# Start of a hybrid encoder step: value weights on a second DMA queue, tile 0 rounded first, identity transposes on PE

## The chip, the cores and the metric

One core of a Trainium2 chip runs the whole program. The metric is the device time in microseconds (us) of one execution, taken as the median of several runs. Engines: PE is TensorE (matrix multiply), ACT is ScalarE, DVE is VectorE, POOL is GpSimd; SP is the sync engine, which here only issues DMAs. A "q" behind an engine's name is its instruction queue.

## What is computed

One layer of a streaming encoder over 1024 prompt tokens and 8 x 16 sample tokens (1152 rows of 1024 features, float32):

```python
def rms_norm(x, w):
    y = xf * lax.rsqrt(jnp.mean(xf * xf, axis=-1, keepdims=True) + EPS)
    return (y * w).astype(x.dtype)

xn = rms_norm(x, norm_w)
h, gb, gc, q, k, v, g_conv, g_attn = jnp.split(xn @ w_in, SPLITS, axis=-1)
...   # q, k: rms_norm per head; short gated convolution of gc * h; sliding-window attention
x = x + merged @ w_out
x = x + (silu(rms_norm(x, w_ffn) @ w_gate) * (rms_norm(x, w_ffn) @ w_up)) @ w_down
```

The change touches only the first some 50 us: the first `rms_norm`, and v, the 256 value columns of `xn @ w_in`.

## The kernel before, in words

The 1152 rows are nine token tiles of 128 rows (`NT = 9`); the 1024 features are eight blocks of 128 (`KT = 8`). Every float32 product is made of three matmuls on operands split into a rounded high part and a remainder (`PASSES`: high x high, high x low, low x high). So every operand is split: ACT makes the high part by a rounding copy, then POOL (weights) or DVE (tokens) subtracts it from the source to make the low part.

Each engine has its own instruction list, in the order written in its block, and the lists meet in semaphores alone. The head of the program, by engine:

- **SP** (lines 371 to 388) issues the loads: x tile 0, the norm weight broadcast to all partitions (`wbc_p`, line 381), value-weight half 0 (`v_half(Slab(0))`, two DMAs of 256 KB into `raw0`), x tile 1, value-weight half 1 (two DMAs into `raw1`), x tiles 2 to 8, then the key weights (`cols`), which wait for a raw buffer to come free. An x tile is 128 rows of 4 KB. A value-weight DMA is 128 partitions x 2 rows of 1 KB. The norm weight is one row of 4 KB, read once for each partition.
- **ACT** (lines 701 to 726): one square root that loads its table (line 703); `norm_stats(0, t)` for a tile is its squares with their sum (line 682) and a root (line 686); `split_hi(Slab(n))` rounds weight half n (line 671); `norm_hi_part(t)` rounds a transposed tile out of PSUM in two halves (line 698); `v_rows(t)` copies a finished value tile (line 711). The order is stats 0, weight half 0, stats 1, then for each t: round tile t, stats t + 2, (at t = 0) weight half 1, and from t = 2 a value copy.
- **DVE** (lines 1006 to 1013): `norm_scale(0, t)` multiplies tile t by 1/rms and the norm weight (lines 989, 995), `norm_lo_part(t)` makes the low part (line 1004). Tiles 0 and 1 are scaled first.
- **POOL**: constants (lines 472 to 485; `consts_made` counts to 11), then `split_lo` of weight halves 0 and 1 (line 490), then small DMAs.
- **PE** (lines 1431 to 1449): `norm_transpose(t)` transposes a normalised tile by eight matmuls against the identity (line 1404, into banks 5 to 7), `v_unit(t, half)` is 12 matmuls of tile t against one weight half (line 1414, bank `t % DU`, `DU = 5`). Tiles 0 and 1 are transposed, then for each t both value halves (tile 0's second half waits for `w_lo >= 2`), and the transposes of tile t + 2. The last four tiles take their second halves afterwards (`V_LATE = 4`). Behind come keys, queries, attention, convolution, output projection (line 1618) and the feed-forward part (lines 1674, 1716).

The normalised tiles have two buffers (`xn_p`), and transposed halves rotate over three banks (`norm_bank`).

Of the kernel before, what the change touches and what calls it, by code (L numbers as in the profile page):

```python
# [32 lines left out]
P = 128  # L33
# [4 lines left out]
NT = TOK // P  # L38
NG = 3
G = TOK // NG  # L40
KT = D // P
HD = 64
NH, NKV = D // HD, 4
NV = NKV * HD
# [7 lines left out]
V_OFF = K_OFF + NKV * HD  # L52
# [19 lines left out]
PASSES = ((0, 0), (0, 1), (1, 0))  # L72

DU = 5

PAIRS = 2 * NCH
RING = 8
# [51 lines left out]
def norm_bank(t, h):  # L129

    return 5 + (2 * t + h) % 3
# [11 lines left out]
def build(nc, io):  # L143
    ctx = ExitStack()
    with ctx:
        def sb(name, shape, dt=F32):
            return ctx.enter_context(nc.sbuf_tensor(name, shape, dt))

        def sem(name):
            return ctx.enter_context(nc.semaphore(name))  # L150
# [56 lines left out]
        raw = [raw0, raw1]  # L207
# [4 lines left out]
        ident = sb("ident", [P, P])  # L212
# [28 lines left out]
        banks = ctx.enter_context(nc.psum_tensor("banks", [P, 8, 512], F32))  # L241
# [5 lines left out]
        raw_in = [sem("raw_in0"), sem("raw_in1")]  # L247
        cache_in = [sem("cache_in0"), sem("cache_in1")]
        wbc_in = sem("wbc_in")
# [33 lines left out]
        w_in = io["w_in"][0].rearrange("(k p) c -> p k c", p=P)  # L283
# [14 lines left out]
        def slab_is_done(eng, kind, idx):  # L298
            if kind == "u":
                eng.wait_ge(gemm_ready, idx)  # L300
            elif kind == "du":
                eng.wait_ge(d_ready, idx)
            elif kind == "f":
                eng.wait_ge(gemm_ready, 3 * (idx + 1))
            else:
                eng.wait_ge(d_ready, NT * (idx + 1))
# [51 lines left out]
        def _(sp):  # L358
            def load(slab, halves_of):


                if not (isinstance(slab.n, int) and slab.n < 2):
                    sp.wait_ge(w_lo, slab.n - 1)
                for dst, src in halves_of:
                    sp.dma_start(dst, src).then_inc(raw_in[slab.slot], 16)
# [5 lines left out]
            def x_tile(t):  # L371
                sp.dma_start(X[:, t, :], xp[t] if t < NT - 1 else xsm).then_inc(x_in[t], 16)

            def v_half(slab):

                k0 = slab.n * KT // 2
                load(slab, [(raw[slab.slot][:, k * NV:(k + 2) * NV].rearrange("p (k c) -> p k c", k=2),
                             w_in[:, k0 + k:k0 + k + 2, V_OFF:V_OFF + NV]) for k in (0, 2)])

            x_tile(0)  # L380
            sp.dma_start(wbc_p[:, :], io["norm_mix_w"][0].partition_broadcast(P)).then_inc(wbc_in, 16)
            v_half(Slab(0))
            x_tile(1)
            v_half(Slab(1))
            for t in range(2, NT):
                x_tile(t)
            cols(Slab(2), w_in, K_OFF)
            cols(Slab(3), w_in, K_OFF + P)
            with sp.Fori(0, 2) as i:
                for j in range(4):  # L390
                    slab = Slab(Q_SLAB + j, 4, i)
# [273 lines left out]
        def _(act):  # L665
            def split_hi(slab, *free):
                act.wait_ge(raw_in[slab.slot], 32 * (slab.turn + 1))
                if free:

                    slab_is_done(act, *free)  # L670
                act.activation(ws[slab.slot][0][:, :], raw[slab.slot][:, :], ACT.Copy).then_inc(w_hi, 1)  # L671

            def norm_squares(ph, t):

                if ph == 0:
                    act.wait_ge(x_in[t], 16)
                else:

                    act.wait_ge(d_free, LAST_BASE + LAST_POS[1, t] + 1)
                act.wait_ge(sq_done, (NT + 6) * ph + t + 1)  # L680
                scratch = scratch_p[:, :] if ph == 0 else junk[:, :] if t < 4 else xn_f[:, 0, :]
                act.activation(scratch, X[:, t, :], ACT.Square, accum_out=ss[:, t:t + 1]).then_inc(sq_done, 1)

            def norm_roots(ph, t0, t1):
                act.wait_ge(sq_done, (NT + 6) * ph + t1 + 1)
                act.activation(sd[:, t0:t1], ss[:, t0:t1], ACT.Sqrt, bias=eps[:, :], scale=1.0 / D).then_inc(sd_done, t1 - t0)

            def norm_stats(ph, t):
                norm_squares(ph, t)
                norm_roots(ph, t, t + 1)  # L690

            def norm_hi_part(t):

                for h in range(2):
                    idx = 2 * t + h
                    act.wait_ge(nT_done, idx + 1)
                    src = banks[:, norm_bank(t, h), :].rearrange("p (k c) -> p k c", k=4)
                    act.activation(xs[0][:, 4 * h:4 * h + 4, t * P:(t + 1) * P], src, ACT.Copy).then_inc(norm_hi, 1)


            act.wait_ge(consts_made, 11)

            act.activation(sd[:, 0:1], eps[:, :], ACT.Sqrt).then_inc(sq_done, 1)
            norm_stats(0, 0)
            split_hi(Slab(0))
            norm_stats(0, 1)

            def v_rows(t):

                act.wait_ge(v_ready, t + 1)  # L710
                act.activation(V[:, 1 + t, :], banks[:, t % DU, 0:NV], ACT.Copy).then_inc(v_done, 1)

            for t in range(NT):
                norm_hi_part(t)
                if t + 2 < NT:
                    norm_stats(0, t + 2)
                if t == 0:
                    split_hi(Slab(1))
                if 2 <= t < NT - V_LATE + 2:
                    v_rows(t - 2)  # L720

# [261 lines left out]
        def _(dve):  # L983
            def norm_scale(ph, t):

                xn, wbc = ((xn_p, wbc_p), (xn_f, wbc_f))[ph]
                q = NT * ph + t
                dve.wait_ge(sd_done, q + 1)
                dve.reciprocal(rms[:, t:t + 1], sd[:, t:t + 1]).then_inc(rms_done, 1)
                if ph == 0 and t >= 2:  # L990
                    dve.wait_ge(nT_done, 2 * (t - 1))
                if ph == 1 and t >= 2:
                    dve.wait_ge(tr_done, 2 * (t - 1))
                dve.wait_ge(rms_done, q + 1)
                dve.scalar_tensor_tensor(out=xn[:, t % 2, :], in0=X[:, t, :], scalar=rms[:, t:t + 1], in1=wbc[:, :],
                                         op0=ALU.mult, op1=ALU.mult).then_inc(xn_ready, 1)

            def norm_lo_part(t):
                for h in range(2):
                    idx = 2 * t + h  # L1000
                    dve.wait_ge(norm_hi, idx + 1)
                    src = banks[:, norm_bank(t, h), :].rearrange("p (k c) -> p k c", k=4)
                    where = (slice(None), slice(4 * h, 4 * h + 4), slice(t * P, (t + 1) * P))
                    dve.tensor_tensor(xs[1][where], src, xs[0][where].bitcast(F32), ALU.subtract).then_inc(norm_lo, 1)

            dve.wait_ge(wbc_in, 16)
            norm_scale(0, 0)
            norm_scale(0, 1)

            for t in range(NT):  # L1010
                norm_lo_part(t)
                if t + 2 < NT:
                    norm_scale(0, t + 2)
            dve.wait_ge(const_in, 16 * 15)
# [176 lines left out]
            def add_rows(s, hf, x_turn=None):  # L1191
                for t in range(NT):
# [4 lines left out]
                    else:  # L1197

                        dve.wait_ge(d_free, NT * (s - 2) + t + 1)
                    dve.tensor_tensor(x, banks[:, 3 + t % DU, :], x, ALU.add).then_inc(d_free, 1)  # L1200

# [176 lines left out]
        def _(pe):  # L1378
# [17 lines left out]
            def norm_transpose(t):  # L1396
                pe.wait_ge(xn_ready, t + 1)
                for h in range(2):
                    idx = 2 * t + h
                    if idx >= 3:  # L1400
                        pe.wait_ge(norm_lo, idx - 2)
                    for k in range(4):
                        kt = 4 * h + k
                        mm = pe.transpose(banks[:, norm_bank(t, h), k * P:(k + 1) * P],  # L1404
                                          xn_p[:, t % 2, kt * P:(kt + 1) * P], ident[:, :])
                    mm.then_inc(nT_done, 1)
# [3 lines left out]
            def v_unit(t, half):  # L1410

                for k in range(KT // 2):
                    for n, (w, x) in enumerate(PASSES):
                        mm = pe.matmul(banks[:, t % DU, 0:NV], xs[x][:, 4 * half + k, t * P:(t + 1) * P],  # L1414
                                       ws[half][w][:, k * NV:(k + 1) * NV],
# [12 lines left out]

            norm_transpose(0)
            norm_transpose(1)
            for t in range(NT):
                pe.wait_ge(norm_lo, 2 * (t + 1))
                if t >= DU:
                    pe.wait_ge(v_done, t - DU + 1)
                if t < 2:
                    pe.wait_ge(w_lo, 1)
                mm = v_unit(t, 0)
                if t < NT - V_LATE:  # L1440
                    if t == 0:
                        pe.wait_ge(w_lo, 2)
                    v_unit(t, 1).then_inc(v_ready, 1)
                elif t == NT - 1:
                    mm.then_inc(v_half_used, 1)
                if t + 2 < NT:
                    norm_transpose(t + 2)
            for t in range(NT - V_LATE, NT):
# [174 lines left out]
            def row_units(slot, s, act_slot):  # L1623
                for t in range(NT):

                    if t >= DU:
                        pe.wait_ge(d_free, NT * s + t - DU + 1)
# [129 lines left out]
```

## Time and profile before

| | us |
|---|---|
| Median of 3 runs | 1736.22 |
| Lowest, highest | 1735.95, 1737.91 |
| The profiled execution's own time | 1736.17 |
| Its span in the profile | 1734.4 |

Busy times in the span: PE 1693.8 us, its weight loads (PEld, beside the matmuls) 1598.8, DVE 891.4, POOL 876.8, ACT 649.2.

How to read it: times of rows are counted from the span's start. "Busy" is the time in which an engine works; an engine waits idle for a semaphore, and a row names what released it behind an arrow. The chain of waits is followed back from the last instruction: at each step to what released it, or to the instruction before it on its engine. A DMA's time to landing runs from its issue to its last byte. The DMA share is the mean busy share of the core's 16 DMA engines, PEclk the clock granted to TensorE.

### The profile page before, as it was taken

The numbers are of one execution on the slowest core, as the hardware profiler recorded it, in microseconds if no ns is written. First come the engines' busy times: TensorE is split into PE (matmuls) and PEld (weight loads), VectorE is DVE, ScalarE is ACT, GpSimd is POOL, SyncE is SP. The second block draws the span as 40 slices with busy tenths as digits, with TensorE's granted clock in tenths as the row PEclk, the third lists the DMA queues.
The fourth block names the chain that finished last, engine by engine and source line by source line (L and its number), as shares of the span: only waits on it lengthen the run. The fifth ranks groups of instructions, "written<-read, shape, count | busy, mean of one in ns | idle before, by whom it ended". The sixth has DMA issues, their size and how long they took to land.

```text
span 1734.4 us, 29336 instructions
## 1 busy us (share of the span) xinstructions
PE 1693.8 (98%) x10942; PEld 1598.8 (92%) x10942; DVE 891.4 (51%) x1537; ACT 649.2 (37%) x1354; POOL 876.8 (51%) x779
## 2 busy tenths in 40 slices
PE   7999999999999999999998999999979999999999
PEld 7999999989999999999887999999969999999998
DVE  5400465536554313312567756657677555565555
ACT  6221555535554211111115454444434333333331
POOL 3412555345552221212235887887848665666662
PEclk9999999999999999999999999999989999999999
DMA  5221111111111111114120334333323223222222
GB/s 172 51 47 48 41 35 35 30 32 48 34 35 32 37 49 37 48 36 155 41 85 25 98 99 121 97 99 97 98 73 122 80 91 98 74 74 74 95 77 85
DMA packets 143155, 121.66 MB, mean 70 GB/s; under 512 B 33202, under 2 KB 124750, under 8 KB 143024
## 3 DMA queue, kind: packets, MB, share of 16 engines
q1 hardware_dynamic: 130400, 115.89, 21.6%
q10 hardware_dynamic: 11984, 3.61, 0.9%
q8 instruction: 81, 1.33, 0.3%
q0 software_dynamic: 640, 0.43, 0.1%
q14 instruction: 50, 0.41, 0.1%
HBM read 114.58 MB, written 5.32 MB: 69 GB/s over the span
## 4 chain that ended last, share of the span: by engine, by line
PE 84%; issue 9%; DVE 3%; POOL 3%; ACT 1%; DMA 0%; SPq 0%; POOLq 0%; DVEq 0%; ACTq 0%
PE banks L1674 28%; PE banks L1391 27%; PE banks L1716 15%; PE banks L1618 5%; PE banks L1560 2%; PE banks L1542 2%; PE banks L1414 1%; POOL w_lo L490 1%; PE banks L1522 1%; PE banks L1567 1%; DVE xc_lo L1245 1%; PE banks L1489 1%; DMA X<-in_x_prompt 0%; PE banks L1531 0%; PE banks L1404 0%
## 5 line engine op out<-in xcount | busy, mean ns | idle before, releaser
L1391 PE MATMUL banks<-x_hi,w_hi 128*128 128x384 f32 x1200 | 412.2, 344 | 0.0
L1391 PE MATMUL banks<-x_hi,w_lo 128*128 128x384 f32 x1200 | 401.8, 335 | 0.0
L1391 PE MATMUL banks<-x_lo,w_hi 128*128 128x384 f32 x1200 | 401.5, 335 | 0.0
L490 POOL TENSOR_TENSOR w_lo<-w_raw,w_hi 128x1024 fp32r<-128x1024 f32 x44 | 113.2, 2573 | 428.9 <-ACT w_hi L671 428.8
L1674 PE MATMUL banks<-xc_hi,ring_a 128*128 128x256 f32 (+1 forms) x1200 | 247.2, 296 | 0.0
L1391 PEld LDWEIGHTS banks<-x_hi,w_hi 128*128 128x128 f32 x1200 | 225.9, 188 | 5.1
L1391 PEld LDWEIGHTS banks<-x_lo,w_hi 128*128 128x128 f32 x1200 | 225.6, 188 | 0.8
L1391 PEld LDWEIGHTS banks<-x_hi,w_lo 128*128 128x128 f32 x1200 | 225.3, 188 | 0.0
L636 POOL TENSOR_TENSOR ring_a<-raw_f,ring_a 128x512 fp32r<-128x512 f32 x133 | 191.5, 1453 | 19.0 <-ACT ring_a L899 17.8
L1674 PEld LDWEIGHTS banks<-xc_hi,ring_a 128*128 128x128 f32 x1200 | 196.4, 190 | 0.4
L1674 PE MATMUL banks<-xc_lo,ring_a 128*128 128x256 f32 (+1 forms) x600 | 177.7, 296 | 0.0
L1329 DVE TENSOR_TENSOR X<-banks,X 128x512 f32<-128x512 f32 x198 | 128.5, 683 | 42.4 <-PE banks L1716 42.4
L1716 PE MATMUL banks<-ring_a,h_act 128*128 128x512 f32 x618 | 144.0, 391 | 1.0 <-DVE X L1329 1.0
L1674 PE MATMUL banks<-xc_hi,ring_o 128*128 128x256 f32 (+1 forms) x640 | 136.8, 300 | 5.2 <-DVE xc_lo L1245 5.2
L1716 PEld LDWEIGHTS banks<-ring_a,h_act 128*128 128x128 f32 x618 | 114.9, 188 | 25.9 <-issue 1.4
L636 POOL TENSOR_TENSOR ring_a<-w_sums,ring_a 128x512 fp32r<-128x512 f32 x63 | 87.6, 1390 | 84.5 <-ACT ring_a L899 84.5
L671 ACT ACTIVATE w_hi<-w_raw 128x1024 fp32r<-128x1024 f32 x60 | 63.4, 1056 | 153.3 <-PE banks L1391 89.8
L1674 PEld LDWEIGHTS banks<-xc_lo,ring_a 128*128 128x128 f32 x600 | 113.9, 190 | 0.4
L1674 PEld LDWEIGHTS banks<-xc_hi,ring_o 128*128 128x128 f32 x640 | 107.5, 193 | 5.8 <-DVE xc_lo L1245 5.6
L899 ACT ACTIVATE ring_a<-raw_f 128x512 fp32r<-128x512 f32 x133 | 81.6, 624 | 78.3 <-PE banks L1716 58.6
L800 ACT ACTIVATE probs<-banks,soft,rs 128x256 f32<-128x256 f32 x144 | 79.7, 562 | 63.6 <-DVE soft L1061 63.5
L636 POOL TENSOR_TENSOR ring_o<-raw_f,ring_o 128x512 fp32r<-128x512 f32 x66 | 93.3, 1423 | 8.7 <-ACT ring_o L899 8.3
(222 smaller groups left out, 3256.7 us busy)
## 6 DMA issues: line engine op xcount, KB each, us to landing
w_raw<-in_w_in SPq DMA_DIRECT2D x104, 256.0 KB, 3.2
raw_f<-in_w_gate SPq DMA_DIRECT2D x88, 256.0 KB, 3.7
raw_f<-in_w_up SPq DMA_DIRECT2D x88, 256.0 KB, 3.7
raw_f<-in_w_down SPq DMA_DIRECT2D x88, 256.0 KB, 3.5
X<-in_x_prompt SPq DMA_DIRECT2D x16, 512.0 KB, 9.3
w_raw<-in_w_out SPq DMA_DIRECT2D x16, 256.0 KB, 3.0
out_y_prompt<-X SPq DMA_DIRECT2D x16, 256.0 KB, 2.1
cache_v_twice<-in_cache_v ACTq DMA_DIRECT2D x34, 64.0 KB, 2.3
```

The costliest lines, as they stand in the source:

```text
L490: gp.tensor_tensor(ws[slab.slot][1][:, :], raw[slab.slot][:, :], ws[slab.slot][0][:, :].bitcast(F32), ALU.subtract).then_inc(w_lo, 1)
L636: gp.tensor_tensor(slot_view(n, 1), slot_source(n), slot_view(n, 0).bitcast(F32), ALU.subtract).then_inc(f_lo, 1)
L671: act.activation(ws[slab.slot][0][:, :], raw[slab.slot][:, :], ACT.Copy).then_inc(w_hi, 1)
L800: act.activation(p[:, h, :], scores[:, h, :], ACT.Exp, bias=soft[:, 2, h:h + 1], scale=scale, accum_out=soft[:, 4, h:h + 1])
L899: act.activation(slot_view(n, 0), slot_source(n), ACT.Copy).then_inc(f_hi, 1)
L1329: dve.tensor_tensor(x, banks[:, 4 + n % 4, :], x, ALU.add).then_inc(y_free, 1)
L1391: mm = pe.matmul(banks[:, bank, 0:G], ws[slot][w][:, kt * P:(kt + 1) * P], xs[x][:, kt, g * G:(g + 1) * G], start=(kt == 0 and n == 0), st ...
L1542: mm = pe.transpose(banks[:, 5 + k, h * P:(h + 1) * P], Pb[:, (3 * t + u) % 2, h, k * P:(k + 1) * P], ident[:, :])
L1560: mm = pe.matmul(banks[HD * e:HD * (e + 1), 7, s * P:(s + 1) * P], vst[:, par, k, HD * s:HD * (s + 1)], PT[:, k, 2 * s + e, :], start=(k = ...
L1618: mm = pe.matmul(banks[:, bank, :], acts[act_slot][:, k, x, t * P:(t + 1) * P], ws[slot][w][:, k * 512:(k + 1) * 512], start=(k == 0 and n ...
L1674: mm = pe.matmul(banks[:, bank, 0:nb], ring(n)[:, w, k * P:(k + 1) * P], xc[x][:, X_OF_PROD[j], k, 0:nb], start=(start and k == 0 and z == 0),
L1716: mm = pe.matmul(banks[:, 4 + n % 4, :], rows, ring(SLOT0[r] + 2 * hf + k)[:, w, :], start=(k == 0 and o == 0), stop=(k == 1 and o == 2))
```

## The change

- `v_half` moves from SP's list to ACT's, where ACT issues the norm weight's DMA and then the four value-weight DMAs before anything else. SP issues the nine x tiles in a row, then the key weights as before.
- ACT's order: after stats 0 and weight half 0 it rounds tile 0, then weight half 1, then makes stats 1 and stats 2. Before, stats 1 came ahead of the rounding of tile 0 and weight half 1 behind stats 2.
- DVE scales tile 1 after the low part of tile 0, not ahead of it.
- PE begins with 24 transposes of the identity into bank 4 (`DU - 1`), whose results nobody reads, then transposes tile 0; tile 1's transposes come behind both value halves of tile 0.

```diff
+WARM = 24
...
@@ SP
-            x_tile(0)
-            sp.dma_start(wbc_p[:, :], io["norm_mix_w"][0].partition_broadcast(P)).then_inc(wbc_in, 16)
-            v_half(Slab(0))
-            x_tile(1)
-            v_half(Slab(1))
-            for t in range(2, NT):
+            for t in range(NT):
                 x_tile(t)
@@ ACT
+            def v_half(slab):
+
+                k0 = slab.n * KT // 2
+                for k in (0, 2):
+                    act.dma_start(raw[slab.slot][:, k * NV:(k + 2) * NV].rearrange("p (k c) -> p k c", k=2),
+                                  w_in[:, k0 + k:k0 + k + 2, V_OFF:V_OFF + NV]).then_inc(raw_in[slab.slot], 16)
+
+            act.dma_start(wbc_p[:, :], io["norm_mix_w"][0].partition_broadcast(P)).then_inc(wbc_in, 16)
+            v_half(Slab(0))
+            v_half(Slab(1))
             act.wait_ge(consts_made, 11)
             act.activation(sd[:, 0:1], eps[:, :], ACT.Sqrt).then_inc(sq_done, 1)
             norm_stats(0, 0)
             split_hi(Slab(0))
-            norm_stats(0, 1)
...
             for t in range(NT):
                 norm_hi_part(t)
+                if t == 0:
+                    split_hi(Slab(1))
+                    norm_stats(0, 1)
                 if t + 2 < NT:
                     norm_stats(0, t + 2)
-                if t == 0:
-                    split_hi(Slab(1))
@@ DVE
             norm_scale(0, 0)
-            norm_scale(0, 1)
             for t in range(NT):
                 norm_lo_part(t)
+                if t == 0:
+                    norm_scale(0, 1)
                 if t + 2 < NT:
                     norm_scale(0, t + 2)
@@ PE
+            for _ in range(WARM):
+                pe.transpose(banks[:, DU - 1, 0:P], ident[:, :], ident[:, :])
             norm_transpose(0)
-            norm_transpose(1)
             for t in range(NT):
...
                 elif t == NT - 1:
                     mm.then_inc(v_half_used, 1)
+                if t == 0:
+                    norm_transpose(1)
                 if t + 2 < NT:
                     norm_transpose(t + 2)
```

## Rows read from the trace of the kernel before

**Rows 1.** The profile's page: busy time of PE and the others, share of the span.

```profile
PE 1693.8 (98%) x10942; PEld 1598.8 (92%) x10942; DVE 891.4 (51%) x1537; ACT 649.2 (37%) x1354; POOL 876.8 (51%) x779
```

**Rows 2.** Busy time by stretch (us), then length, engines, granted clock, DMA share, GB/s.

```profile
0.00:20.00 20.00, 9.00 (x47) 8.34 (x48) 8.53 (x12) 11.20 (x21) 9.19 (x22) 1.00 0.93 332
85.00:190.00 105.00, 104.81 (x631) 103.78 (x630) 6.28 (x16) 25.64 (x49) 31.39 (x33) 1.00 0.19 47
```

**Rows 3.** Chain of waits, 0 to 60 us: start, duration (us), what.

```profile
3.69 0.52 SPq L365
...
14.52 2.91 POOL w_lo L490
...
20.30 2.88 PE banks L1414 x24
```

**Rows 4.** Timeline, first 16 us: start, duration, engine, line, operation [idle before <-releaser].

```profile
0.81 1.28 ACT L703 ACT_TABLE_LOAD   x1 [0.81 <-PEq L1746]
...
2.21 0.09 POOL L485 MEMSET ones<- 64x1 f32 x1
...
4.08 1.06 ACT L682 ACTIVATE scratch_p<-X 128x1024 f32<-128x1024 f32 x1 [1.53 <-DMA X<-in_x_prompt]
...
6.44 0.16 DVE L989 RECIPROCAL rms<-sd 128x1 f32<-128x1 f32 x1 [6.44 <-DMA wbc_p<-in_norm_mix_w]
...
9.10 2.35 POOL L490 TENSOR_TENSOR w_lo<-w_raw,w_hi 128x1024 fp32r<-128x1024 f32 x1 [6.79 <-ACT w_hi L671]
...
10.62 1.06 ACT L698 ACTIVATE x_hi<-banks 128x512 fp32r<-128x512 f32 x2
...
12.02 1.06 ACT L682 ACTIVATE scratch_p<-X 128x1024 f32<-128x1024 f32 x1 [0.33 <-DMA X<-in_x_prompt]
...
13.90 1.28 DVE L995 SCALAR_TENSOR_TENSOR xn_p<-X,rms,wbc_p 128x1024 f32<-128x1024 f32 x1
...
15.10 1.28 DVE L1004 TENSOR_TENSOR x_lo<-banks,x_hi 128x512 fp32r<-128x512 f32 x2
```

**Rows 5.** DMA issues at 4.2 to 4.6, then 7.0 to 7.5 us: KB each, us to landing.

```profile
w_raw<-in_w_in SPq DMA_DIRECT2D x1, 256.0 KB, 7.0
...
X<-in_x_sample SPq DMA_DIRECT2D x1, 512.0 KB, 12.4
```

**Rows 6.** Busy time by stretch again, 2 to 4 us; the last number is GB/s.

```profile
2.00:4.00 2.00, 0.00 (x0) 0.00 (x0) 0.00 (x0) 0.29 (x2) 0.25 (x4) 1.00 0.96 328
```

**Rows 7.** DMA queues, 190.5 to 190.7 us: packets, MB, engine time (q1 SP, q10 ACT).

```profile
q1 hardware_dynamic: 86, 0.04, 71.4%
q10 hardware_dynamic: 83, 0.02, 46.1%
```

**Rows 8.** SP's DMA queue at 17 to 18, 8.8 to 9.3 and 4.2 to 5.2 us.

```profile
q1 hardware_dynamic: 116, 0.41, 103.2%
...
q1 hardware_dynamic: 196, 0.19, 108.1%
...
q1 hardware_dynamic: 51, 0.21, 92.2%
```

**Rows 9.** Timeline of PE, 12 to 20.4 us, columns as in rows 4.

```profile
12.58 1.97 PE L1404 MATMUL banks<-ident,xn_p 128*128 128x128 f32 x8 [2.57 <-DVE xn_p L995]
...
14.56 0.41 PE L1414 MATMUL banks<-w_hi,x_lo 128*128 128x256 f32 x1
14.77 0.41 PE L1414 MATMUL banks<-w_lo,x_hi 128*128 128x256 f32 x1
...
18.06 0.28 PE L1414 MATMUL banks<-w_lo,x_hi 128*128 128x256 f32 x1
...
19.26 1.03 PE L1404 MATMUL banks<-ident,xn_p 128*128 128x128 f32 x8
...
20.05 0.36 PE L1414 MATMUL banks<-w_hi,x_hi 128*128 128x256 f32 x1
```

More of the change, by code:

```diff
@@ L372, in x_tile @@
                 sp.dma_start(X[:, t, :], xp[t] if t < NT - 1 else xsm).then_inc(x_in[t], 16)
[L374 to L378, printed above, removed]
-            x_tile(0)
-            sp.dma_start(wbc_p[:, :], io["norm_mix_w"][0].partition_broadcast(P)).then_inc(wbc_in, 16)
-            v_half(Slab(0))
-            x_tile(1)
-            v_half(Slab(1))
-            for t in range(2, NT):
+            for t in range(NT):
                 x_tile(t)
```

## The prediction

> **What bounds the kernel now.** I read the busy shares first. TensorE (PE) is busy for 98% of the span [rows 1]. The table of stretches shows where the rest lies: 9.00 of the first 20 us are busy, later 104.81 of 105 [rows 2]. So the head is empty by 11 us, and behind it PE has next to no slack. Whatever moves the point from which PE runs without a gap moves the end by the same amount, and the later stages neither absorb nor multiply it.
>
> That point is the second value tile: its first matmul starts at 20.05 us [rows 9], and from there on the chain of waits names PE alone, 2.88 us for 24 matmuls [rows 3]. Ahead of it the chain runs through x tile 2's DMA, ACT's squares and root [rows 4], the rounding of the second weight half, POOL's subtraction (14.52 to 17.43) and PE [rows 3]. POOL's 2.91 us is what PE's second half of the first tile waits for. So the quantity to forecast is the start of the second value tile, called S2 here: 20.05 now.
>
> **The change part by part.** *The same bytes, two queues.* The landings now are: x0 at 4.0 us, the norm weight at 6.4 and x2 at 12.0, where ACT and DVE stop waiting for them [rows 4]; the second half of the value weights at 3.69 + 7.0 = 10.7, and the last x tile, issued between 7.0 and 7.5 with 12.4 us to landing, at about 19.7 [rows 3, 5]. The order of SP's queue put the 1 MB of value weights ahead of all but two of the nine x tiles. At 17 to 18 us one queue alone moves 410 GB/s with the engines' time full (103.2%) [rows 8], so a second queue cannot add bytes. After the change nine x tiles stand in SP's queue and the norm weight and four weight DMAs in ACT's, and what decides is how the 16 engines share themselves between two queues.
>
> *How they share.* The trace has one view of both queues backlogged: at 190.5 to 190.7 us SP's queue carries a weight load in packets of about 512 bytes (0.04 MB in 86 packets) and ACT's a cache load in packets half as large (0.02 MB in 83) [rows 7]. That is one packet each in turn: sharing by bytes would give ACT two packets for each of SP's, and turns of a whole DMA would give SP about two for each of ACT's (256 KB / 512 B = 512 packets in a DMA against 64 KB / 256 B = 256).
>
> At the start the same turn-taking meets unequal packets. An x row is 4 KB, a value weight row 1 KB: 0.41 MB in 116 packets against 0.19 MB in 196 [rows 8]. Those rows give 0.16 us per 4 KB packet and engine (16 engines / 100 packets per us) and 0.043 us per 1 KB packet. The norm weight, one row read 128 times, is slower: 51 packets per us, 0.31 us each [rows 8]. Per engine SP's queue holds 9 x 8 = 72 packets and ACT's 8 + 64 = 72 as well, so **the second weight half lands when the last x tile does**. From the first bytes at 1.8: eight turns of 0.16 + 0.31 end at 5.6; 32 turns of 0.16 + 0.043 end at 12.2; 32 more at 18.7. Half a us from data to landing, an estimate from x0 (between 2 and 4 us 0.66 MB move [rows 6], and x0's 0.5 MB, first in the queue, are in at 4.0), gives x0 and norm weight 6.1, first half 12.7, second half 19.2. The cross-check is today's last x tile, 19.7, behind the same bytes. Bounds for the second half: 18.4 (the norm weight costs no more than any row) to 19.8.
>
> The Trainium skill (DMA: Bandwidth & Descriptors, "Issuing engines are not separate DMA queues") speaks against this part: queues share the same 16 engines and a second one saves only issue time. Here an issue on SP takes 0.52 us [rows 3], and the trace agrees that there is little else to save. The same page ("Queues, rings and completion order") says that an engine drains a whole packet of typically 9 to 17 descriptors from a ring before it switches; read so, it is the second rival below, and 86 against 83 packets [rows 7] speaks against it.
>
> *ACT's order.* ACT issues five DMAs (5 x 0.5 us), and its table load (1.28 us, now at 0.81 [rows 4]) comes behind or ahead of them. Either order ends by 4.8, before x0 at 6.1, so it costs nothing. Ahead, ACT's packets start 1.3 us later, within the bound of 19.8. Then ACT runs: statistics of tile 0, rounding of half 0, rounding of tile 0, rounding of half 1, statistics of tiles 1 and 2. Tile 0 reaches PE 3.1 us after its landing (as x2: 12.02 to 13.90 + 1.28 [rows 4]), at 9.2. Half 0 is rounded 12.7 to 13.8, tile 0 until 14.8 (1.06), DVE's low part until about 15.5 (0.64 behind), POOL's half 0 (2.35) until 16.2 [rows 4]. So the first 12 value matmuls run 16.3 to 18.9; now they run around 14.56 [rows 9]. This alone is still no loss, because they wait for half 1 anyway.
>
> *Half 1 is the price.* ACT waits for it with the statistics of tiles 1 and 2 queued behind. Landing 19.2; rounding 1.06, until 20.3; POOL 2.40 (2.35 at best, 2.90 as now), until 22.7; the second 12 matmuls from 22.75. PE has then been idle since 18.9. Its granted-clock column reads 1.00 everywhere, but matmuls start 0.21 us apart at 14.6 (the 1.2 GHz level) and 0.12 us apart later (2.88 / 24, 2.4 GHz) [rows 3], one of 0.28 us standing first at 18.06; and after the idle time before 12.58 eight transposes took 1.97 us instead of 1.03 [rows 9]. So I take these 12 at 0.21, until 25.35. Tile 1's normalised rows are ready 3.2 us after its statistics begin (x2 again), at 23.5, no limit.
>
> *Tile 1's transposes, moved behind.* They stood before the first value matmuls, in idle time. Now they stand between the two value tiles: 1.03 us fast or 1.97 slow, 1.45 taken, until 26.8. Their second half is then rounded (0.53), subtracted (0.64) and handed over (0.1) [rows 4]: S2 = 28.1. All fast: 27.4; all slow: 28.6. Tile 2's transposes fit beside that.
>
> *The 24 transposes on PE.* They start once POOL has made the constants, which by its last memset is 2.3 us [rows 4], and take at most 24 x 0.25 = 5.9 us [rows 9], until 8.2, before tile 0 arrives at 9.2. They cost nothing, and if tile 0 came at 7.2 they would cost up to 0.9. The clock they earn would speed tile 0's transposes by 0.9 us, but ACT is waiting for half 0 until 12.7, and PE idles for 6 us after them. Worth zero.
>
> *Sum.* 28.1 - 20.05 = +8.0 us. With the landing between 18.4 and 19.8, POOL between 2.35 and 2.90 and the clock both ways: +6.4 to +9.7. The profiled run took 1736.17, its span 1734.4, and the median of three is 1736.22, so both bases agree. Forecast **1744.2 us** (+0.46%), own range 1742.6 to 1745.9.
>
> **The rivals.** *A, even bytes, faster.* If the queues shared by bytes, x0 and the norm weight would be in at 6.1, half 0 one MB later (2.6 us) at 8.7, half 1 at 11.3. POOL's half 1 would end at 11.3 + 1.06 + 2.4 = 14.8, and S2 = 14.85 + 2.1 (12 matmuls, clock rising midway) + 1.0 + 1.3 = 19.3: **-0.8 us, 1735.4**. It decides the sign: S2 is 7.2 to 9.4 us behind half 1's landing, so only a landing before 10.7 to 12.8 is no loss, and today's landing is 10.7. Against it: [rows 7]. For it: the queues there carry smaller packets, and no 4 KB packet is seen sharing an engine. Even then there's no gain over 0.2%, since that asks for a landing at 8 or earlier.
>
> *B, turns of a whole DMA.* x0 4.0, norm weight 6.4, then an x tile (1.3) and a weight DMA (0.7) in turn: half 0 at 10.4, half 1 at 14.4. S2 = 14.4 + 1.06 + 2.4 + 1.95 + 1.0 + 1.4 = 22.2: **+2.1 us, 1738.3**. Against it again [rows 7].
>
> *C, it does not do what it says.* ACT's table load goes first and delays its packets; the total of bytes still ends both queues together, at most 0.6 us later. It lies inside my own range.
>
> **How the numbers follow.** Own case with C: 0.70. A: 0.12. B: 0.12. A worse stall than I have (a clock that stays low into the second tile): 0.03. A gain that I have no mechanism for: 0.03. The range 1737.3 to 1746.3 takes in my case and B, 0.82, and leaves A out. A measurement of this kernel tells about 0.2% (3.5 us) from no change: slower 0.73, within 0.24 (A and B), faster 0.03.
>
> **What would show it.** Right: the second rounding of value weights on ACT starts near 19 us, POOL's after 20, the first value matmuls near 16 at 0.21 us spacing, and PE without gaps from 28; packets of 1 and 4 KB equal in number between 7 and 18 us. Wrong: ACT's weight DMAs land 8 us or less after issue (A, B), or a later stage of PE shrinks by what the head lost, against [rows 2].

## The result, and the profile after

The changed kernel takes 1744.03 us (median of 6 runs, 1743.09 to 1745.12) against 1736.13 (6 runs) before: ratio 1.0048, 95% interval 1.0037 to 1.0058. It is slower by 7.9 us, 0.48%, and the interval lies wholly above 1. The profiled execution took 1743.09 us, its span is 1741.3.

The chain of waits of the changed kernel, 0 to 60 us (start, duration, what); it answers to [rows 3]:

```profile
0.81 0.41 ACTq L699
...
2.83 16.61 DMA w_raw<-in_w_in
...
19.47 1.07 ACT w_hi L662
...
20.60 2.36 POOL w_lo L481
...
23.00 2.47 PE banks L1416 x12
25.48 1.69 PE banks L1406 x8
...
27.19 0.61 ACT x_hi L689
...
27.82 0.70 DVE x_lo L1005
...
28.57 3.14 PE banks L1416 x24
```

The chain is now one DMA, the last of ACT's four weight DMAs: issued from 2.83, 16.61 us to landing, where the same transfer took 7.0 us before [rows 5]. Behind it ACT, POOL, PE, and then one round through transposes, rounding and subtraction of tile 1, before the second value tile starts at 28.57. That start is called S2 throughout; it was 20.05 before [rows 9].

The DMA queues of the changed kernel (q1 SP, q10 ACT: packets, MB, engine time) at 7 to 9 and at 7 to 18 us; they answer to [rows 7, 8]:

```profile
q1 hardware_dynamic: 184, 0.63, 78.3%
q10 hardware_dynamic: 180, 0.18, 26.3%
...
q1 hardware_dynamic: 960, 3.47, 79.5%
q10 hardware_dynamic: 956, 0.93, 24.5%
```

The two queues send equal numbers of packets over all these 11 us, and the queue with 4 KB rows gets 3.5 to 3.7 times the bytes. At 7 to 9 us they move 0.82 MB together, 410 GB/s, the same as one queue before. Equal counts alone do not tell how many packets an engine takes in one turn. But x tile 0 is only eight packets for each engine. SP's packets came first (18 at 1.8 to 2.1 us, none of ACT's), and still the tile landed two us later than before (6.10 against 4.08), so a turn was shorter than those eight.

Timeline of the changed kernel, columns as in [rows 4]:

```profile
2.36 4.84 PE L1434 MATMUL banks<-ident 128*128 128x128 f32 x24 [2.36 <-POOL ones L476]
...
6.10 1.06 ACT L673 ACTIVATE scratch_p<-X 128x1024 f32<-128x1024 f32 x1 [1.20 <-DMA X<-in_x_prompt]
...
9.22 1.35 PE L1406 MATMUL banks<-ident,xn_p 128*128 128x128 f32 x8 [2.02 <-DVE xn_p L996]
...
13.18 1.06 ACT L662 ACTIVATE w_hi<-w_raw 128x1024 fp32r<-128x1024 f32 x1 [5.60 <-DMA w_raw<-in_w_in]
...
16.81 0.55 PE L1416 MATMUL banks<-w_hi,x_hi 128*128 128x256 f32 x1 [6.24 <-POOL w_lo L481]
17.16 0.41 PE L1416 MATMUL banks<-w_hi,x_lo 128*128 128x256 f32 x1
17.38 0.41 PE L1416 MATMUL banks<-w_lo,x_hi 128*128 128x256 f32 x1
```

PE sits idle for 6.24 us behind tile 0's transposes, and the value matmuls then start 0.21 us apart (17.16, 17.38), at the slow level; the granted clock of 10 to 20 us is 0.50 (last section).

### The profile page after: what moved, and what is told of

The parts are those of the page before. It is cut to its first block, busy times and chain, and to the rows that moved or that the text cites. A ratio compares the mean times of both kernels' runs of the same rounds, so it can differ in the third digit from the quotient of the medians.

```text
span 1741.3 us, 29383 instructions
## 1 busy us (share of the span) xinstructions
PE 1699.0 (98%) x10966; PEld 1603.2 (92%) x10966; DVE 892.3 (51%) x1537; ACT 650.6 (37%) x1354; POOL 876.8 (50%) x779
## 4 chain that ended last, share of the span: by engine, by line
PE 83%; issue 9%; POOL 3%; DVE 3%; DMA 1%; ACT 1%; ACTq 0%; POOLq 0%; SPq 0%; DVEq 0%
PE banks L1679 27%; PE banks L1393 27%; PE banks L1721 15%; PE banks L1623 5%; PE banks L1565 2%; PE banks L1547 2%; PE banks L1416 1%; POOL w_lo L481 1%; PE banks L1527 1%; DMA w_raw<-in_w_in 1%; PE banks L1572 1%; PE banks L1494 1%; DVE xc_lo L1247 0%; PE banks L1406 0%; PE banks L1536 0%
```

## The experiments

All kernels are compared by three marks: S2 in the profiled execution; the start of the 324 output-projection matmuls that stand in one piece in the chain (830.51 before); and the median time as a ratio to runs of before on the same chip. Medians of different rows can come from different chips, so times are compared by the ratios; "difference" is the second mark less S2. S2 is read from PE's timeline; in a chain of waits a piece starts only where the one before it ends, up to 0.25 us later. What each is: E1 the queue alone, E2 the orders and transposes alone, E3 the change without its 24 transposes, E4 the change with SP's later tiles held back, E5 with small x packets, E7 E1 with tile 1's transposes late, E6, E8, E9 and E10 versions of E2 in search of a faster one.

| Kernel | S2 | 324 matmuls from | difference | median | ratio to before (95%) |
|---|---|---|---|---|---|
| before | 20.05 | 830.51 | 810.5 | | |
| changed | 28.57 | 839.19 | 810.6 | 1744.03 | 1.0048 (1.0037 to 1.0058) |
| E1 | 25.20 | 837.44 | 812.2 | 1741.27 | 1.0032 (1.0021 to 1.0043) |
| E2 | 19.95 | 832.10 | 812.2 | 1735.70 | 0.9998 (0.9989 to 1.0008) |
| E3 | 29.02 | 839.58 | 810.6 | 1743.77 | 1.0043 (1.0026 to 1.0060) |
| E4 | 20.70 | 832.76 | 812.1 | 1736.28 | 1.0003 (0.9993 to 1.0012) |
| E5 | 22.25 | 834.34 | 812.1 | 1738.10 | 1.0014 (1.0005 to 1.0023) |
| E7 | 28.57 | 840.77 | 812.2 | 1743.08 | 1.0042 (1.0026 to 1.0057) |
| E6 | 18.54 | 830.54 | 812.0 | 1734.73 | 0.9995 (0.9986 to 1.0004) |
| E8 | 18.61 | 829.28 | 810.7 | 1733.15 | 0.9989 (0.9980 to 0.9998) |
| E9 | 17.57 | 828.00 | 810.4 | 1732.95 | 0.9987 (0.9978 to 0.9997) |
| E10 | 19.11 | 829.85 | 810.7 | 1734.24 | 0.9992 (0.9983 to 1.0001) |

### E1: the queue alone

```diff
 # kernel before; ACT issues the norm weight and v_half(0), v_half(1); SP:
-            x_tile(0)
-            sp.dma_start(wbc_p[:, :], ...)
-            v_half(Slab(0))
-            x_tile(1)
-            v_half(Slab(1))
-            for t in range(2, NT):
+            for t in range(NT):
                 x_tile(t)
```

> The kernel before, with nothing changed but the queue: norm weight and value weights are issued by ACT, the orders of ACT, DVE and PE are the old ones, no transposes ahead. Theory (packets taken in turn starve ACT's queue of 1 KB rows): the second weight half lands at 19.2 to 19.6 us, its rounding starts then, POOL ends it near 23, tile 1 is transposed beforehand, and the second value tile (S2, 20.05 before) starts at 23.0 + 1.4 to 2.6 + 0.9 to 1.9 = 25.4 to 27.2; time +5.5 to +7 us, 1741.5 to 1743. Rival (the loss comes from the new orders and tile 1's moved transposes): landing may be late, but S2 stays within 1 us of 20.05 and the time at 1736.

Its chain of waits:

```profile
3.31 15.98 DMA w_raw<-in_w_in
...
19.32 1.07 ACT w_hi L660
...
20.45 2.38 POOL w_lo L479
...
22.88 1.70 PE banks L1413 x12
24.57 0.87 PE banks L1403 x8
```

The landing and POOL's end are the theory's. S2 (25.20) and the time (1741.27) are each 0.2 below the ranges that it gave. So the queue alone costs 5.15 us of head, and the rest of the change adds 3.4.

### E2: the orders and the transposes alone

```diff
 # changed kernel; norm weight and value weights back on SP in the old order
-            act.dma_start(wbc_p[:, :], ...)
-            v_half(Slab(0))
-            v_half(Slab(1))
```

> The changed kernel with the loads back in SP's queue in the old order; the new orders of ACT, DVE and PE and the 24 transposes stay. Theory: the second half lands at 10.7 again, POOL ends it near 14.3, S2 comes at 18.5 to 19.5, time -0.5 to -1.5 us (1734.6 to 1735.6), within noise of before. Rival (orders and moved transposes cost): S2 at 24 or later, time above 1740.

The loss is gone (0.9998), so with the loads in their old queue the new orders are no loss. But S2 is 19.95, not 18.5 to 19.5, and the time of 1735.70 is 0.1 above its range. I had let PE's clock rise in time. Its chain of waits shows 24 value matmuls that take 5.68 us (0.21 us apart and a gap), in spite of 24 transposes that ran until 7.6 us and tile 0's until 9.0; the granted clock of 11.7 to 17.3 us is 0.50:

```profile
11.65 5.68 PE banks L1417 x24
17.32 0.63 PE banks L1407 x4
```

### E3: without the 24 transposes

```diff
-            for _ in range(WARM):
-                pe.transpose(banks[:, DU - 1, 0:P], ident[:, :], ident[:, :])
```

> The changed kernel without its 24 transposes of the identity. Theory: worth zero, since PE waits for the first weight half from 10.6 to 16.8 anyway: tile 0's eight transposes take 1.95 us instead of 1.35, the first value matmuls still start at 16.8, S2 at 27.5 to 28.8, time within 1 us of the changed kernel (1743 to 1745). Rival (they keep the clock up later, or they are in the way): S2 moves by over 1 us.

The time is 1743.77 against 1744.03 (ratios 1.0043 and 1.0048): in the changed kernel they are worth nothing that can be measured, as forecast. S2 lies at 29.02, 0.2 past the top of the expected range and 0.45 later than with them. The chain shows where, in PE alone:

```profile
22.97 2.93 PE banks L1416 x12
25.90 3.15 PE banks L1406 x16
```

Without the 24 transposes all 12 matmuls of the second half are slow, 2.93 us against 2.47 in the changed kernel, and the 16 transposes of tiles 1 and 2 behind them are slow too. In the changed kernel the first four of the 12 run at the fast level (last section). That is 0.45 us of head in one profiled execution each.

### E4: SP's later tiles held back

```diff
             for t in range(NT):
+                if t == 2:
+                    sp.wait_ge(raw_in[1], 32)
                 x_tile(t)
```

> The changed kernel with one wait more on SP: x tiles 2 to 8 are issued only when the second weight half has landed, so that ACT's queue has the engines nearly alone. Theory: the second half lands at 10 to 10.5 us instead of 19.4, x2 at about 12.8, S2 at 18.8 to 20, time 1735 to 1736, so the whole loss is gone although ACT's queue and all orders stay. Rival (issuing from ACT or its queue is slow by itself): the half lands no earlier than 15, and with x2 behind it S2 is at 25 or later.

DMA queues at 7 to 9 us, then POOL's row in the timeline:

```profile
q10 hardware_dynamic: 732, 0.71, 101.6%
q1 hardware_dynamic: 26, 0.04, 5.4%
```

```profile
10.28 4.69 POOL L483 TENSOR_TENSOR w_lo<-w_raw,w_hi 128x1024 fp32r<-128x1024 f32 x2 [7.97 <-ACT w_hi L664]
```

ACT's queue moves 0.71 MB in 2 us when it is alone, four times the 0.18 MB that it got beside 4 KB packets. ACT waits for the first half and rounds it from 9.14. The second half is in before ACT comes to it: SP, which waits for its landing, issues again at 10.56, and ACT rounds it from 11.06 without a wait. POOL's two subtractions stand back to back (x2). S2 at 20.70 is 0.7 past its range (matmuls at the slow spacing again) and the time of 1736.28 is 0.3 past its own, but the loss is gone within the noise (1.0003, 0.9993 to 1.0012) with ACT's queue and every new order in place. What was slow was not the issuing from ACT but the sharing with SP's backlog.

### E5: small packets for x

```diff
+            x_tile(0)
+            for t in (1, 3, 5):
+                for c in range(0, D, 256):
+                    dst, src = X[:, t:t + 2, c:c + 256], xp[t:t + 2, :, c:c + 256].rearrange("t p d -> p t d")
+                    sp.dma_start(dst, src).then_inc(x_pair[t // 2], 16)
+            for t in (7, 8):
                 x_tile(t)
```

> The changed kernel with x tiles 1 to 6 fetched in packets of 1 KB instead of 4 KB: each pair of tiles by four DMAs of 256 columns (tile 0, 7, 8 as they were). Same bytes, same two queues, same orders on every engine. Theory (one packet each in turn): ACT's 64 weight packets per engine now alternate with 1 KB packets, 64 x 0.09 us behind 5.5 us, so the second half lands at 11 to 12 us instead of 19.4, and S2 (28.57 in the changed kernel) comes at 19.5 to 21; time 1735 to 1737. Rival (the queues share bytes or time by some other rule, and packet size is beside the point): the half still lands at 17 or later, time 1742 or more.

DMA queues of this kernel at 7 to 9, then 5 to 7 us, and the rounding of the second half:

```profile
q10 hardware_dynamic: 401, 0.39, 56.5%
q1 hardware_dynamic: 387, 0.37, 52.3%
...
q1 hardware_dynamic: 263, 0.26, 46.6%
q10 hardware_dynamic: 153, 0.24, 41.8%
```

```profile
13.13 1.06 ACT L668 ACTIVATE w_hi<-w_raw 128x1024 fp32r<-128x1024 f32 x1 [0.99 <-DMA w_raw<-in_w_in]
```

Packets are again equal in number, and now bytes are too. The half lands at 13.1 instead of 19.4, with the same bytes in the same two queues. The edit also cuts six x DMAs into twelve, but the equal packet counts say that it is the size of the packets that moved the landing, by 6.3 us. The landing is 1.1 us past its range, S2 (22.25) 1.3 us and the time (1738.10) 1.1 us past theirs. At 7 to 9 us the rate is the one I reckoned with. At 5 to 7 us the two queues together move only 0.50 MB, 250 GB/s, where 400 would have brought 0.3 MB more, 0.75 us; the norm weight's last packets and the first small x packets stand there, and I didn't follow it further.

### E7: where the other 3.4 us are

```diff
 # E1, and on PE:
             norm_transpose(0)
-            norm_transpose(1)
...
+                if t == 0:
+                    norm_transpose(1)
```

> The queue-only kernel (S2 at 25.20, 1741.3) with one thing more, PE's transposes of tile 1 behind both value halves of tile 0. ACT and DVE keep the old orders. It tells how the 3.4 us between the queue-only kernel and the changed one divide. Theory (tile 1's transposes and the rounding behind them now stand on the path): matmuls of the second half end at 24.6 as there, 8 transposes 0.9, rounding 0.6, subtraction 0.7: S2 at 26.7 to 27.5 if the clock stays up, up to 28.5 if it falls; time 1742.5 to 1744. Rival (the orders of ACT and DVE cost the 3.4 us): S2 stays at 25 to 25.5.

Chain of waits:

```profile
22.96 2.93 PE banks L1413 x12
25.89 0.68 PE banks L1403 x4
...
26.60 0.61 ACT x_hi L687
...
27.23 0.70 DVE x_lo L1003
...
27.98 0.66 PE banks L1403 x4
28.63 3.08 PE banks L1413 x24
```

Against E1 only PE's list differs, and S2 moves from 25.20 to 28.57: moving tile 1's transposes costs 3.4 us. That S2 is the changed kernel's to the hundredth is chance, because two things differ between them. E7 has neither the new orders of ACT and DVE nor the 24 transposes. E3 stands between: the new orders take S2 from 28.57 (E7) to 29.02 (E3), and the 24 transposes bring it back to 28.57. So the orders of ACT and DVE cost at most 0.45 us of head here. In both E7 and E3 the 12 matmuls take 2.93 us; behind them PE makes 12 transposes in 1.74 us in E7, but 16 in 3.35 us in E3. In E7 ACT makes tile 1's statistics ahead of rounding tile 0, and PE's first value matmuls run at 18.98 to 21.9 instead of 16.8 to 19.7, with 1.06 us of idle time behind them instead of 3.29.

About 1.2 of the 3.4 us go with the clock: the second half's matmuls take 2.93 us here against 1.70 in E1, where tile 1's transposes had put PE to work from 17.62 on. The other 2.1 us lie behind them: four transposes of tile 1, its rounding and subtraction, and then the last four of tile 2, which the program lets wait until the low part of tile 1's first half is made, since three banks serve the four halves (`norm_bank`). S2 lies 0.1 above my upper end for a falling clock.

### E6, E8, E9, E10: a version that beats both

E6 is E2 with 20 transposes of the identity behind tile 0's and 8 between the value halves; E8 is E6 with both weight halves ahead of x tile 1, and six transposes between the value halves instead of eight; E9 is E6 with tile 1's transposes between the value halves, its statistics ahead of the second rounding, and 4 fillers behind; E10 is E9 without any identity transposes.

```diff
 # E9 against E2
+            def fill(n):
+                for _ in range(n):
+                    pe.transpose(banks[:, DU - 1, 0:P], ident[:, :], ident[:, :])
+            fill(WARM)
             norm_transpose(0)
+            fill(20)
...
+                        norm_transpose(1)
+                        fill(4)
                         pe.wait_ge(w_lo, 2)
...
-                if t == 0:
-                    norm_transpose(1)
...   # ACT
-                    split_hi(Slab(1))
                     norm_stats(0, 1)
+                    split_hi(Slab(1))
```

> The order-only kernel (loads on SP in the old order, S2 at 19.95) with 20 more identity transposes behind tile 0's and 8 between the two value halves, so that PE isn't idle before the first value matmuls. Theory (the clock fell because PE was idle from 8.96 to 11.65, after which 24 matmuls ran 0.21 us apart): they now run 0.12 us apart, S2 at 18.0 to 18.8, time -0.8 to -1.7 us (1734.2 to 1735.2). Rival (clock isn't held by such work, or the transposes delay the value matmuls): matmuls still 0.21 us apart, S2 at 20 or later.

> As the kernel before it with 6 transposes between the halves, and SP issues both weight halves ahead of x tile 1. Theory: the second half lands at 9.5 instead of 10.8, its rounding starts when tile 0 is rounded (10.05), POOL ends it at 13.8, x1 lands at 10.9 in time: S2 at 17.3 to 18.2, time -1.5 to -2.5 us (1733.4 to 1734.5), the fastest version if any is. Rival (x1 becomes the last to come: its statistics are queued behind): S2 no earlier than in the kernel before it.

> The fill kernel (loads on SP in the old order, S2 at 18.54) with tile 1's transposes between the two value halves, where PE has only filler transposes today, and ACT making tile 1's statistics ahead of rounding the second half (x1 lands at 9.2, the half at 10.8). Four filler transposes behind tile 1's. Theory (tile 1's transposes and the rounding behind them are the last thing on the path, 1.7 to 2.5 us of it): tile 1's transposes run at 13.6 to 14.5, the second half's matmuls 15.0 to 16.5, S2 at 17.2 to 17.8; against before -2.3 to -2.8 us of the head, time 1732.5 to 1733.5. Rival (POOL's second half, pushed back by 0.7 us, eats it): S2 at 18.3 or later.

> The kernel of the run before without any transposes of the identity (neither the 24 nor the fillers): the orders alone. Theory (the slow clock in the first value tile costs about what the fillers gain): transposes and the first value matmuls at 0.21 to 0.24 us each until about 18 us, S2 at 18.5 to 19.5, so 1.0 to 1.9 us behind the filled kernel and 0.5 to 1.5 ahead of before; time 1734 to 1735.3. Rival (the fillers do nothing for the end): S2 within 0.5 us of the filled kernel.

Chain of waits of E9:

```profile
12.47 2.73 POOL w_lo L492
...
15.24 1.70 PE banks L1417 x12
16.94 0.87 PE banks L1407 x8
17.81 2.87 PE banks L1417 x24
```

E6's mechanism held: with PE kept at work the 12 matmuls take 1.70 us at 14.40, and S2 moves from 19.95 to 18.54; its time does not leave the noise (0.9995, up to 1.0004). E8's theory fell. S2 is 18.61, no earlier than E6's. The second half came earlier, but POOL had no time for it. The first half was rounded only from 8.54 instead of 8.03, and from then on POOL's two subtractions are back to back until 14.4:

```profile
9.68 4.72 POOL L492 TENSOR_TENSOR w_lo<-w_raw,w_hi 128x1024 fp32r<-128x1024 f32 x2 [7.37 <-ACT w_hi L673]
```

The 1.6 us by which its median lies below E6's are not from the head: in the profiled executions 1.3 us of difference come at 388 us (last section), and 1.7 more behind the 324 matmuls. E9 comes out as written, S2 17.57, and has the lowest ratio of the study: 0.9987 (0.9978 to 0.9997), 2.9 us below before by the medians. E8's 0.9989 lies inside that interval. E10 shows what of the head is order and what is clock: 0.9 us by order (20.05 to 19.11) and 1.5 by the identity transposes (19.11 to 17.57). The difference in time between E9 and E10 (1.3 us) lies inside their intervals.

## Why the prediction was right, point by point

The forecast was 1744.2 us, the result 1744.03. The mechanism, how the two queues share, was right; that the two numbers agree to 0.2 us was helped by errors that cancel: the head moved by 0.5 us more than forecast, and the later stages gave a part of it back.

- **How the queues share** was the step on which all hung, and it held at a size that the trace of before had not shown: 184 against 180 packets at 7 to 9 us, 960 against 956 at 7 to 18. The sign followed from it. Rival A needed equal bytes (0.63 against 0.18 MB is not that). Rival B needed turns of whole DMAs, with landings at 10.4 and 14.4; E5 made the bytes equal by small packets and took 6.3 us off the landing.
- **Landings**: x0 6.1 forecast, 6.10 by ACT's row; first half 12.7, rounding at 13.18; second half 19.2, rounding at 19.47.
- **The path behind it**: POOL's end 22.7 forecast, 22.96; matmuls from 22.75, 23.00; S2 28.1, 28.57. Of the 0.5 us that S2 is late, 0.25 came in with the landing. Rival C's open point settled the harmless way: ACT issued first, the table load followed.
- **The 24 transposes** at zero: E3 confirms it for the time. They ended at 7.2, and the 0.6 us that they took off tile 0's transposes (1.35 against 1.94 us in E3) was swallowed by the wait for the first half. The 0.45 us by which S2 comes earlier with them is a part of the clock's history that the sum did not have.
- **The orders of ACT and DVE** at nothing by themselves: that is right to 0.45 us of head (E7 against E3), and E2 shows no loss in time with them.
- **The second half's matmuls** were taken at 2.60 us, all slow. They took 2.47, because four of them were fast. All slow they take 2.93 (E3, E7), so this term was 0.3 us too small, and the fast spell hid it.
- **The term that I had too small** is the round of tile 1 through PE, ACT and DVE: from the end of the second half's matmuls to S2 it takes 28.57 - 25.47 = 3.10 us, not 2.75 (1.45 + 1.27 and the start of the next), the transposes being at the slow clock to their end (1.69 of the chain). What I had not seen is that its old place also kept the clock up: E7 against E1 prices the move at 3.4 us, 1.2 of it the slow matmuls that my sum put down to the idle time alone.
- **"Tile 2's transposes fit beside that"** held by little: the last four of them end at 28.41, and S2 comes 0.16 us later. In E3, with slow transposes, they are what S2 waits for.
- **"The later stages neither absorb nor multiply it" was not quite right.** S2 moved by 8.52 us, the 324 matmuls by 8.68, but the last 120 matmuls only from 1703.99 to 1710.92, by 6.93. The median moved by 7.9. The 1.8 us go between two marks of the chains: the piece that starts at 1232.81 before starts at 1241.58 (8.77 later), the one at 1309.23 starts at 1316.20 (6.97 later). PE is far from full there. Before, at 1240 to 1312 us (length, PE busy, then the others):

```profile
1240.00:1312.00 72.00, 58.78 (x341) 52.13 (x340) 56.64 (x72) 28.57 (x44) 46.18 (x30) 0.91 0.26 88
```

I had read "next to no slack" from the 98% and from one stretch, 85 to 190 us. But PE is idle for 40.6 us of the span, 11 in the head and 13.2 in this stretch alone. That my 8.0 agrees with 7.9 to a tenth is luck at this level.

## What to carry to other kernels

Here a second DMA queue added no bandwidth (410 GB/s with either), and beside a backlog it changed who got the bandwidth: both queues sent equal numbers of packets (960 and 956), so the queue with the shorter rows got the smaller share. Before moving an urgent transfer to a queue of its own, compare row sizes and the backlog of the other queue, or keep the urgent one ahead in the same queue (E2), or hold the backlog back (E4). And a step moved "into a gap" is only free if the gap exists in the new order: tile 1's transposes left idle time and entered the path, for 3.4 us (E1 to E7). In E9 they stand between the two value halves, where PE waits for POOL anyway, and S2 is 1.0 us earlier than in E6.

## What the runs showed of the hardware that I had not expected

**One clock fall far behind the change divides the profiled executions.** The difference column of the table takes two values, 810.4 to 810.7 and 812.0 to 812.2. Around 388 us PE waits for ACT (2.10 us in before, 2.61 in E2), and what follows differs. Busy time by stretch (the number after the last bracket is the granted clock) for before at 388 to 392, E2 at 388 to 392, and the changed kernel at 396.6 to 400.6:

```profile
388.00:392.00 4.00, 3.88 (x34) 3.71 (x35) 2.72 (x6) 3.10 (x9) 3.92 (x10) 1.00 0.47 137
```

```profile
388.00:392.00 4.00, 3.88 (x26) 3.74 (x27) 2.71 (x6) 2.52 (x7) 3.92 (x10) 0.70 0.35 95
```

```profile
396.60:400.60 4.00, 3.85 (x34) 3.68 (x35) 2.72 (x6) 2.75 (x9) 3.92 (x10) 1.00 0.36 98
```

Before and the changed kernel have 34 matmul records there, E2 26 in the same 4 us. In all six kernels with 812 the granted clock of the 4 us behind the wait is 0.61 to 0.70, in all six with 810.5 it is 1.00. But two of the latter, E3 and E9, have a fall as well, ahead of the wait: E9 has a granted clock of 0.53 at 379.6 to 382.8, and E3:

```profile
390.90:394.00 3.10, 3.10 (x11) 3.10 (x11) 1.56 (x3) 1.72 (x2) 1.86 (x2) 0.52 0.01 3
```

There PE waits less for ACT, 1.05 us in E3 and 0.73 in E9 instead of 2.1 to 2.8, and the start of the 324 matmuls does not move. So in these traces a fall behind the wait costs about 1.6 us and one ahead of it nothing that the difference column shows. The length of the wait alone does not decide whether the clock falls behind it: 2.26 us in E1 with a fall, 2.77 in E8 without. Each kernel has one profiled execution, so it is open whether the fall belongs to the kernel or to the execution, and what turns it on was not tested. It makes 1.3 us between the profiled executions of E6 and E8, whose heads are alike.

**PE's clock level lags behind its work in both directions.** In the changed kernel the first matmul at 23.00 and those behind it stand at the fast spacing (0.12 us from 23.46 to 23.58), after 3.29 us of idle time and slow matmuls ahead of that; from 23.58 on the spacing is 0.21 again (start, duration; then stretches with the granted clock third from the end):

```profile
23.00 0.39 PE L1416 MATMUL banks<-w_hi,x_hi 128*128 128x256 f32 x1 [3.29 <-POOL w_lo L481]
...
23.46 0.31 PE L1416 MATMUL banks<-w_hi,x_hi 128*128 128x256 f32 x1
23.58 0.40 PE L1416 MATMUL banks<-w_hi,x_lo 128*128 128x256 f32 x1
```

```profile
10.00:20.00 10.00, 3.47 (x15) 2.80 (x13) 1.29 (x2) 2.56 (x4) 2.35 (x1) 0.50 1.05 385
20.30:23.00 2.70, 0.00 (x0) 0.00 (x0) 1.04 (x2) 2.64 (x7) 2.40 (x2) 1.00 0.08 19
23.60:26.90 3.30, 3.30 (x18) 3.30 (x17) 1.79 (x3) 0.53 (x1) 3.30 (x8) 0.50 0.65 183
```

The clock is at half speed while the first 12 value matmuls run, at full speed in the gap, where PE does nothing, and at half speed again soon after PE is back at work. So work ahead of a gap can make the clock fast in the gap, where it is of no use. In these runs filler work paid where it reached up to 0.3 or 0.9 us before the work it was meant for (E6, E9, E8); where 2.5 to 2.7 us of idle time stood between (E4, E2), the matmuls were slow. The column can be trusted only from its first change on: before, it reads 1.00 at 8 to 17.4 us, while matmuls stand 0.21 us apart.

**A broadcast of one row delays what shares the engines with it.** Before, the norm weight moved alone at 210 GB/s, 51 packets in a us [rows 8]. In the changed kernel it shared the engines with x tile 0: at 3 to 5 us they sent 76 and 73 packets, 305 GB/s together, where plain rows reach 410. x0, which had landed at 4.08 [rows 4], landed at 6.10: two more us for the first thing that the kernel needs, hidden here only by the greater delay behind it. In E5 the same two transfers made 91 packets each in the same 2 us, 373 GB/s; why was not followed.
